# Adaptive-norm parameters of layer 0: fewer computed ahead of the layer, the others inside its later stages

## The reference

```python
mods = (jax.nn.silu(cond) @ lw['w_ada'] + lw['b_ada'])[:, None, :]
shift1, scale1, gate1, shift2, scale2, gate2 = jnp.split(mods, 6, axis=-1)
h = rms_norm(x, lw['norm1_gain']) * (1 + scale1) + shift1
# h @ w_in -> pooling mixer, neighbourhood attention, gated linear attention
x = x + gate1 * (jnp.concatenate([y_pool, y_na, y_la], axis=-1) @ lw['w_out'])
h2 = rms_norm(x, lw['norm2_gain']) * (1 + scale2) + shift2
x = x + gate2 * swiglu(h2, lw['w_ffn_in'], lw['w_ffn_out'])
```

## Time and profile before

| | |
|---|---|
| median of 3 runs | 1791.59 us (1788.95 to 1792.82) |
| profiled execution | 1790.72 us, of it 1788.9 us span from the first to the last instruction |
| PE busy | 1680.8 us (94%), granted clock 0.97 of full on average |
| DVE, POOL, ACT busy | 1081.2 us, 625.6 us, 540.7 us |
| DMA | 171.45 MB, mean 96 GB/s |

### The profile page before, as it was taken

How to read it: one execution, slowest core, us unless ns; L and a number is a source line. 1 busy time by engine, 2 the same in 40 slices (tenths; PEclk the granted TensorE clock), 3 DMA queues, 4 the chain that set the end, 5 groups by cost and what they waited for, 6 DMA issues and landing times.

```text
span 1788.9 us, 27647 instructions
## 1 busy us (share of the span) xinstructions
PE 1680.8 (94%) x11424; PEld 1616.0 (90%) x11424; DVE 1081.2 (60%) x1890; ACT 540.7 (30%) x890; POOL 625.6 (35%) x295
## 2 busy tenths in 40 slices
PE   3798899999999999999979789998999999999997
PEld 3687789889999999999979778887999999999997
DVE  7887688956787588757647855556644413341341
ACT  2332244344222122112334125444332212221232
POOL 3135212126343433344452431111533333333335
PEclk9898899999999999999989889999999999999999
DMA  9410133312343454343231002221222222222212
GB/s 360 148 60 14 51 124 124 112 36 95 118 150 134 141 177 141 130 157 136 70 116 48 27 27 66 71 72 35 65 68 81 72 71 77 77 71 73 81 60 95
DMA packets 49901, 171.45 MB, mean 96 GB/s; under 512 B 6320, under 2 KB 9072, under 8 KB 49392
## 3 DMA queue, kind: packets, MB, share of 16 engines
q1 hardware_dynamic: 49776, 169.68, 28.2%
HBM read 165.86 MB, written 3.80 MB: 95 GB/s over the span
## 4 chain that ended last, share of the span: by engine, by line
PE 83%; DVE 12%; issue 2%; ACT 2%; DMA 2%; SPq 0%; POOL 0%; DVEq 0%; ACTq 0%
PE acc L1300 54%; PE acc L1283 13%; PE bank_S L1408 2%; PE acc L1320 2%; PE banks_OX L1434 2%; PE banks_OX L1467 1%; DVE banks_OX L784 1%; PE banks_OX L1508 1%; PE bank_P L1422 1%; PE bank_S L1450 1%; PE bank_S L1409 1%; PE banks_OX L1436 1%; DVE tmp L1069 1%; PE banks_OX L1471 1%; PE banks_OX L1362 1%
## 5 line engine op out<-in xcount | busy, mean ns | idle before, releaser
L513 POOL TENSOR_TENSOR w_lo<-w_raw,w_hi 128x1024 fp32r<-128x1024 f32 (+1 forms) x196 | 508.0, 2593 | 1050.8 <-ACT w_hi L591 1050.7
L591 ACT ACTIVATE w_hi<-w_raw 128x1024 fp32r<-128x1024 f32 (+1 forms) x196 | 205.4, 1049 | 659.1 <-PE acc L1300 458.1
L1300 PE MATMUL acc<-h_hi,w_hi 128*128 128x320 f32 (+1 forms) x1440 | 331.1, 311 | 0.5 <-DVE means L1233 0.5
L1300 PE MATMUL acc<-h_lo,w_hi 128*128 128x320 f32 (+1 forms) x1440 | 331.2, 311 | 0.0
L1300 PEld LDWEIGHTS acc<-h_hi,w_hi 128*128 128x128 f32 x1440 | 243.1, 189 | 2.5 <-issue 0.9
L1300 PEld LDWEIGHTS acc<-h_lo,w_hi 128*128 128x128 f32 x1440 | 242.6, 189 | 0.0
L1300 PE MATMUL acc<-h_hi,w_lo 128*128 128x320 f32 (+1 forms) x1440 | 231.0, 313 | 0.0
L1300 PEld LDWEIGHTS acc<-h_hi,w_lo 128*128 128x128 f32 x1440 | 220.1, 190 | 0.0
L1193 DVE SCALAR_TENSOR_TENSOR x<-acc,mods,x 128x320 f32<-128x320 f32 (+2 forms) x192 | 72.6, 434 | 213.0 <-PE acc L1300 201.8
L1300 PE MATMUL acc<-y_hi,w_hi 128*128 128x320 f32 x808 | 183.9, 308 | 0.0
L1300 PE MATMUL acc<-y_lo,w_hi 128*128 128x320 f32 x808 | 183.9, 308 | 0.0
(11 more groups left out here) (245 smaller groups left out, 2257.8 us busy)
## 6 DMA issues: line engine op xcount, KB each, us to landing
w_raw<-in_w SPq DMA_DIRECT2D x176, 512.0 KB, 3.6
mod_w<-in_w_ada SPq DMA_DIRECT2D x72, 512.0 KB, 3.7
bias<-in_bias SPq DMA_DIRECT2D x16, 576.0 KB, 4.8
w_ada<-in_w_ada SPq DMA_DIRECT2D x16, 512.0 KB, 10.4
w_raw<-in_w SPq DMA_DIRECT2D x16, 384.0 KB, 3.1
w_ada<-in_w_gate SPq DMA_DIRECT2D x8, 512.0 KB, 8.6
x<-in_x SPq DMA_DIRECT2D x1, 2560.0 KB, 9.9
out_x<-x SPq DMA_DIRECT2D x1, 2560.0 KB, 7.5
```

The lines of the kernel that those rows point to most:

```text
L513: pool.tensor_tensor(w_lo[p][:, 0:n], raw[p][:, 0:n], w_hi[p][:, 0:n].bitcast(F32), ALU.subtract).then_inc(lo_made[p], 1)
L591: act.activation(w_hi[p][:, 0:n], raw[p][:, 0:n], ACT.Copy).then_inc(hi_made[p], 1)
L1300: mm = pe.matmul(acc[p][:, half, 0:rows.shape[1]], w[:, k * P:(k + 1) * P], rows, start=w is w_hi[p] and k == 0 and m is hi, stop=w is w_l ...
```

## The change

- Ahead of layer 0, DVE computes 8 rows (`scale1`) and PE 8 columns (`shift1`). Each has a slot of its own, so that no load waits for a slot, and `x` is loaded behind two rows and one column. The constants that are not needed for the norm are loaded behind the first two weight tiles, with a semaphore `rest_in`, on which POOL waits before its first `w_lo`.
- The 16 rows inside the attention stage are now `gate1` and `scale2`.
- The 8 rows of `shift2` move into the output projection of layer 0: two behind `h_lo` of tile 0, one behind that of each of tiles 1 to 6. Behind the last, three small DVE instructions add `b_ada` and write columns T and T+1 (`shift_columns`). PE waits for these (`shift_made`) before the first matmul of `T_FF`.

```diff
-NROWS = 16
-ROW_SLOTS, COL_SLOTS = 8, 2
+NROWS = NCOLS = KT
...
-MOD_ROWS = [(0, SHIFT2 + n) for n in range(2 * KT)]
+MOD_ROWS = [(0, first + n) for first in (GATE1, SCALE2, SHIFT2) for n in range(KT)]
 FIRST_MOD_STEP = 12
+SHIFT2_ROWS = (2, 1, 1, 1, 1, 1, 1, 0)
...
             def load_row(n):
-                if n >= ROW_SLOTS:
-                    sp.wait_ge(mod_used, 2 * (n - ROW_SLOTS + 1))
-                sp.dma_start(ada[n % ROW_SLOTS][:], a["w_ada"][n]).then_inc(ada_in[n % ROW_SLOTS], 16)
+                sp.dma_start(ada_rows[n][:], a["w_ada"][SCALE1 + n]).then_inc(row_in[n], 16)
...
+            load_row(0)
+            load_col(0)
+            load_row(1)
+            sp.dma_start(x[:], a["x"]).then_inc(x_in, 16)
+            for n in range(2, NROWS):
                 load_row(n)
...
+                load_col(n - 1)
+            load_col(NCOLS - 1)
+            for m, t in (("mats", mats), ("b_ada", b_ada), ("small", small_all)):
                 sp.dma_start(t[:], a[m]).then_inc(par_in, 16)
...
                     load(t)
+                    if l == 0 and t == T_K:
+                        for m, dst in (("rope", rope), ("causal", causal), ("heads4", heads4), ("edges", edges),
+                                       ("inv_w", inv_w), ("state", state_in)):
+                            sp.dma_start(dst[:], a[m]).then_inc(rest_in, 16)
...
                 for t in range(T_OUT, T_FF + 2):
                     load(t)
+                    if l == 0 and t >= T_OUT + 2:
+                        for _ in range(SHIFT2_ROWS[t - T_OUT - 2]):
+                            load_mod(mods_loaded)
+                            mods_loaded += 1
...
-            pool.wait_ge(par_in, 16 * NPAR)
+            pool.wait_ge(rest_in, 16 * NREST)
...
                 if l == 0:
-                    link(mods_done(rows_done, 0, SHIFT2, SHIFT2 + 2 * KT))
-                    prepare_second()
+                    mods_done(rows_done, 0, GATE1, GATE1 + KT)
+                    link(mods_done(rows_done, 0, SCALE2, SCALE2 + KT))
+                    second_gains()
                 for m in range(KT):
...
                     ins.then_inc(raw_lo, 1)
+                    if l == 0:
+                        for _ in range(SHIFT2_ROWS[m]):
+                            for s in range(2):
+                                mod_product(rows_done, s, products)
+                            rows_done += 1
+                        if m == KT - 2:
+                            link(mods_done(rows_done, 0, SHIFT2, SHIFT2 + KT))
+                            shift_columns()
                 finish_root("n2")
...
                         if t == T_FF:
+                            pe.wait_ge(shift_made, l + 1)
                             pe.wait_ge(acc_free[0], 1 + acc_uses(l, t))
```

More of the change, by code:

```diff
@@ L55 @@
 WN = NT // 2
-NPAR = 9
+NPAR, NREST = 3, 6
 LRW = 32
@@ L252, in build @@
         with ExitStack() as first:
-            ada = [sb(f"w_ada{s}", [P, KT * P], F32, first) for s in range(ROW_SLOTS + COL_SLOTS)]
+            ada_rows = [sb(f"ada_row{n}", [P, KT * P], F32, first) for n in range(NROWS)]
+            ada_cols = [sb(f"ada_col{n}", [P, KT * P], F32, first) for n in range(NCOLS)]
         with ExitStack() as first:
@@ L286, in build @@
         S, PT, O, X = (bank[n] for n in "SPOX")
-        x_in, par_in, cond_in, cond_made, layer_in = (sem(n) for n in ("x_in", "par_in", "cond_in", "cond_made", "layer_in"))
-        ada_in = [sem(f"ada_in{s}") for s in range(ROW_SLOTS + COL_SLOTS)]
+        x_in, par_in, rest_in, cond_in, cond_made, layer_in = (
+            sem(n) for n in ("x_in", "par_in", "rest_in", "cond_in", "cond_made", "layer_in"))
+        row_in, col_in = [sem(f"row_in{n}") for n in range(NROWS)], [sem(f"col_in{n}") for n in range(NCOLS)]
         ada_cols_used = sem("ada_cols_used")
@@ L383, in load_row @@
             def load_row(n):
-                if n >= ROW_SLOTS:
-                    sp.wait_ge(mod_used, 2 * (n - ROW_SLOTS + 1))
-                sp.dma_start(ada[n % ROW_SLOTS][:], a["w_ada"][n]).then_inc(ada_in[n % ROW_SLOTS], 16)
+                sp.dma_start(ada_rows[n][:], a["w_ada"][SCALE1 + n]).then_inc(row_in[n], 16)
             def load_col(n):
[L389 to L394, removed]
-                load_row(n)
[L396 to L405, removed]
+                sp.dma_start(ada_cols[n][:], a["w_shift1"][n]).then_inc(col_in[n], 16)
+            load_row(0)
[3 more added lines that the diff above has]
+            for n in range(2, NROWS):
+                load_row(n)
+                load_col(n - 1)
+            load_col(NCOLS - 1)
+            for m, t in (("mats", mats), ("b_ada", b_ada), ("small", small_all)):
                 sp.dma_start(t[:], a[m]).then_inc(par_in, 16)
[L407 to L410, removed]
             def load_mod(r):
@@ L437, in _ @@
                     if l == 0:
-                        for r in range(2, 2 * KT):
-                            if t == 11 + r * 3 // 5:
+                        for r in range(2 * KT):
+                            if t == (5 if r < 2 else 11 + r * 3 // 5):
                                 load_mod(r)
@@ L783, in _ @@
                         dve.wait_ge(mod_used, 2 * n + s)
-                    dve.scalar_tensor_tensor(out=products, in0=ada[n % ROW_SLOTS][:], scalar=1.0,
+                    dve.scalar_tensor_tensor(out=products, in0=ada_rows[n][:], scalar=1.0,
                                              in1=cond_rows[:, s, :], op0=ALU.mult, op1=ALU.mult,
-                                             accum_out=mods_of_layer[0][:, n, s:s + 1]).then_inc(mod_used, 1)
+                                             accum_out=mods_of_layer[0][:, SCALE1 + n, s:s + 1]).then_inc(mod_used, 1)
             dve.wait_ge(mod_used, 2 * NROWS)
@@ L901, in _ @@
                 norm()
+                dve.wait_ge(rest_in, 16 * NREST)
                 dve.wait_ge(tile_done[0], 1 + slot_uses(l, T_LR) + 1)
@@ L1259, in _ @@
             pe.wait_ge(cond_made, 1)
-            for n in range(NMID - NROWS):
-                slot = ROW_SLOTS + n % COL_SLOTS
-                pe.wait_ge(ada_in[slot], (n // COL_SLOTS + 1) * 16)
+            for n in range(NCOLS):
+                pe.wait_ge(col_in[n], 16)
                 for k in range(KT):
-                    mm = pe.matmul(acc[0][:, 0, 2 * n:2 * n + 2], ada[slot][:, k * P:(k + 1) * P], cond[:, k, :],
+                    mm = pe.matmul(acc[0][:, 0, 2 * n:2 * n + 2], ada_cols[n][:, k * P:(k + 1) * P], cond[:, k, :],
                                    start=k == 0, stop=k == KT - 1)
@@ L1617, in layout @@
     a["w_ada"] = i["w_ada"].transpose(0, 2, 1).reshape(DEPTH * NMOD, P, D)
-    a["w_gate1"] = tiles(i["w_ada"][0][:, NROWS * P:NMID * P])
+    a["w_shift1"] = tiles(i["w_ada"][0][:, SHIFT1 * P:(SHIFT1 + KT) * P])
     a["b_ada"] = i["b_ada"].reshape(DEPTH * NMOD, P).T
```

29 lines of the change are left out of this document (15 added, 14 removed).

## The result

The changed kernel takes **1803.38 us** (median of 6 runs, 1800.70 to 1806.59), the kernel before 1791.53 (6 runs beside them). The ratio is 1.0065, with a 95% interval of 1.0053 to 1.0077: slower by 11.85 us. The prediction was 1797 us with a range up to 1802. The side was right, the size not: 11.85 us slower where it said 5.5, and just outside its range.

The account below looks back on a forecast made before the run. PE bounds nearly the whole span and the output projection, DVE the stretch ahead of layer 0. 1790.7 - 17.5 (start) + 21.4 (output projection) + 2.5 (clock) = 1797.1, forecast 1797 us; own range 1792 to 1802, stated range 1781 to 1802.

Parts of the forecast that it names:

- PE needs 0.22 us for a matmul of a column: Ahead of layer 0: a column's eight matmuls take 1.7 us on PE, so the last column is done at 36.
- DVE stays the bound: Ahead of layer 0: the root is ready before DVE, whose products end at 43.4.
- The term: Start, ahead of layer 0: first weight tile at 53.9 instead of 71.45, -17.5 us (-16 to -18.7).
- The other steps at the start: Ahead of layer 0: `x` lands at 18.0, third row at 19.3, additions end at 36.3, DVE's products at 43.4.
- Small instructions beside `w_lo`: Norm's tail ahead of layer 0: DVE's small instructions pass beside POOL; by the skill's rule the whole 1 us is lost.
- The output projection: Layer 0: products beside POOL put DVE behind, updates 9.43 us apart, `T_FF` waits for the columns: +21.4 us.
- The clock at `T_FF`: After PE idles 11.5 us, `T_FF` starts at half clock: +2.5 us (+2.1 to +2.8); shorter gaps in tiles 0.
- Attention was put at 0: Attention stage of layer 0: 16 rows as before, other ones, so 0 us.
- A: Output projection: DVE keeps its place, products never wait, `T_FF` loses 2.0 us, 1775 us; chance 8%.
- B: Output projection: `w_lo` falls beside the update and the wait for `h_hi`, updates 7.2 us apart, 1783 us; chance 10%.
- C: Start: 16 loads at once make `x` or row blocks as late as before, gain only 8, 1806 us; chance 3%.
- D: Output projection: PE runs at 1.2 GHz through the gaps, a tile takes 14.1 us, 1811 us; chance 5%.

Follow-up runs that it names:

- half-columns kernel: Changed kernel with the columns summing only every second block of k, four matmuls instead of eight per column, all loads kept: 1795.43 us.
- the sums in another place: Norm's sums on PE put ahead of its last three columns, on the kernel with one second-shift row moved from output-projection tile 0 into attention: 1783.48 us.
- one row behind each tile: Changed kernel with the second row of output-projection tile 0 moved into attention (17 rows there), so each tile but the last has one: 1789.32 us.
- The product that read PSUM: Changed kernel with the output projection's products reading their second input from PSUM instead of SBUF and writing over their row: 1787.07 us.
- the kernel without the second shift's rows: Changed kernel with the eight `shift2` rows of layer 0 left out, no loads or products, the shift zero: 1775.68 us.
- the shorter memset: Changed kernel with one more DVE instruction, a memset of 128x400 ahead of layer 0's first scaling: 1802.26 us.
- the 21 rows in attention: Changed kernel with 21 of its 24 rows in attention and one each behind output-projection tiles 0, 1 and 2: 1786.37 us.

## Why the prediction was wrong in size

**The step that failed: "PE needs 0.22 us for a matmul of a column (6.96 over 32), 1.7 us for eight: 36."** The x32 of that row are records, and each of these matmuls is shown as two. The 32 were two columns, not four: 3.48 us for one. Right is 16 records a column, 3.44 us in the changed kernel, eight columns 27.5. So the columns end at 44.4 instead of 36, the norm's sums start at 44.27 instead of 36.3, and the root comes behind DVE, not ahead of it: "DVE stays the bound" failed with it. The half-columns kernel gave the forecast's 53.9 back (53.87; that it agrees to 0.1 us is luck, as the products ended 0.4 earlier there and the tail took 0.4 more), and so did the sums in another place (53.95). The term is -12.3 instead of -17.5, 5.2 us, and outside the 16 to 19 that the prediction itself named as the sign. By stages, the profiled 1806.3 lies 9.2 over the forecast: 5.2 from this step, 3.9 from attention, 1.7 from the rest and 0.3 from `T_FF`, less 1.9 in the output projection; the median lies 6.3 over it.

The other steps at the start held. DVE's products ended at 43.0 (forecast 43.4), `x` landed at 17.75 (18.0), the third row was there at 19.05 (19.3), the additions ended at 35.0 (36.3). The 358 GB/s of the Trainium skill ("DMA: Bandwidth & Descriptors", "Specifications") would have put that row 2 us later, at 21.3; the trace doesn't agree.

**Small instructions beside `w_lo`** were counted as free. In the changed kernel they ran before `w_lo`, so it didn't matter. Where they meet it, they wait: `COPY` 128x23 took 2.12 us and the gains 2.26 in the half-columns kernel, the sum of 128x16 took 2.36 with one row behind each tile, and alone they take 0.16 to 0.18. The tail there is 10.9 us (43.0 to 53.87) against 9.9 before, which is the whole 1 us that the rule named. The Trainium skill ("SBUF — State Buffer", section "Who interferes with whom") says that VectorE meets GpSimd with a second SBUF input, or with a copy in a mode that uses both ports, and not with one SBUF input alone. The product that read PSUM (1.22 us inside `w_lo`) agrees.

**The output projection** went nearly as forecast. The first product 3.42 us, tile 1's update 12.86 us behind tile 0's (forecast 13.3), the others 9.19 apart (forecast 9.43), `T_FF` behind DVE and an idle PE: +19.5 for +21.4. Within a period the turns come one instruction earlier than forecast: the addition holds up `h_lo` (2.39 us), `w_lo` the first product, and the second is free, where the prediction had the two products held up. The sum is nearly the same, and that is in part luck. Its cause is shown from two sides, by the order (one row behind each tile) and by the input (PSUM): each takes away 15.5 of the 19.5. What remains, 4 us, is mostly the columns' sum that waits 2.36 us for `w_lo` in the one, and tile 0's two rows in the other (10.56 us to the next update instead of 7.04); with three rows it is 0. What tipped the order was the second row of tile 0, as the prediction had it.

**The clock at `T_FF`**: +2.76 for +2.5, and 6.23 where the wait is gone. Within the tiles the granted clock fell once, to 0.65 from 419.1 to 424.0, behind a gap of 1.89 us; PE's wait for the next update shrank to 0.35 us, and the period stayed (9.17 us). So it cost nothing there, as the prediction had it.

**Attention was put at 0**, and took 3.9 us more in the profile, twice. Between kernels whose instructions there are the same it went from 322.1 to 327.6 us, the granted clock's mean from 0.94 to 0.92, and against the kernel without the second shift's rows all of it is longer matmuls. The mean alone doesn't give the length: the shorter memset has 0.94 and 325.0 us. What puts the stretches of lower clock where they are stays open, and so does whether they fall there in every execution of the changed kernel. A forecast should leave such a stage some 2.5 us either way.

The rivals: A fell, as the four products of tile 0 do throw DVE out of its place. B's order is real, but needs one row less there. C and D did not occur: `x` was early, and the tiles ran at 1.00 but for one stretch of 4.9 us.

## What to carry to other kernels

Count the records of a known piece of work before dividing by them: two loads, 32 records, so 16 each. When a bound is taken away at the start, list what every other engine has still to do in order, not only how long its pieces take: here the norm's sums stood behind 27.5 us of columns. And a product like these beside GpSimd's `w_lo` is cheap if one input is in PSUM (1.22 us), or if it is placed where GpSimd has just finished; moving it elsewhere pays only where the engine that runs it has slack, as the 21 rows in attention showed.

## What the runs showed that was not expected

A stage can take longer with the same instructions: attention took 327.6 us in both profiles of the changed kernel, and 322.1 to 322.6 in three kernels whose attention is the same. Adding an instruction of 0.4 or 1.0 us ahead of it made the whole 1.1 us faster, less than these medians tell apart. And a tiny instruction can cost as much as a large one: 2.36 us for a sum of 128x16, where it alone takes 0.16.
